# Moving small steps between engines around the recurrent stage and the attention of a two-layer hybrid trunk

## The reference, cut to what matters

```python
# mixer A: per query the 256 best admissible keys by an index score, then attention over these
score = where(admissible, sum_h w[q,h] * relu(q_idx . k_idx), -inf)
_, idx = lax.top_k(score, topk)        # of equal scores the earlier key wins
p = softmax(where(valid, q_lat . c_kv[idx], -inf))
o_lat = p @ c_kv[idx];  y_a = o_lat @ w_uv
# mixer B: gated delta rule over chunks of 64 rows
S = S * exp(g_last) + k^T (u - w S);   o = (q exp(g)) S + attn (u - w S)
y_b = rmsnorm(o) * silu(z)
# both
h = h + concatenate([y_a, y_b]) @ w_out
```

## Time and profile before

| what | value |
|---|---|
| median of three runs | 2384.43 us |
| the profiled execution's own time | 2382.29 us |
| its span in the trace | 2380.3 us |
| PE busy | 2322.6 us, 98% |
| DVE, ACT, POOL busy | 1654.0, 1022.7, 534.0 us |
| granted TensorE clock, mean | 0.993 of full |

### The profile page before, as it was taken

How to read it: one execution, slowest core, us unless ns; L and a number is a source line. 1 busy time by engine, 2 the same in 40 slices (tenths; PEclk the granted TensorE clock), 3 DMA queues, 4 the chain that set the end, 5 groups by cost and what they waited for, 6 DMA issues and landing times.

```text
span 2380.3 us, 33751 instructions
## 1 busy us (share of the span) xinstructions
PE 2322.6 (98%) x12906; PEld 1835.8 (77%) x12906; DVE 1654.0 (69%) x2671; ACT 1022.7 (43%) x1807; POOL 534.0 (22%) x504
## 2 busy tenths in 40 slices
PE   9999999988999999999999999989999999999998
PEld 6587778864577888888888867767878888888887
DVE  5388787788656977676755587546688777765557
ACT  5323325755633433333333454456343333333344
POOL 5026544311100234333330000000005333331000
PEclk9999999999999999999999999999999999999999
DMA  6121100010043355455596621101335455468663
GB/s 185 47 71 53 45 27 20 3 37 1 28 141 134 116 186 170 157 177 161 192 323 194 195 62 49 49 28 54 115 119 198 149 171 177 143 207 302 205 194 126
DMA packets 236271, 298.26 MB, mean 125 GB/s; under 512 B 13424, under 2 KB 175232, under 8 KB 227024
## 3 DMA queue, kind: packets, MB, share of 16 engines
q1 hardware_dynamic: 220848, 207.66, 28.3%
q0 software_dynamic: 15264, 88.45, 9.9%
HBM read 206.95 MB, written 88.60 MB: 124 GB/s over the span
## 4 chain that ended last, share of the span: by engine, by line
PE 89%; DVE 6%; ACT 3%; issue 2%; POOL 0%; DVEq 0%; ACTq 0%; POOLq 0%
PE ps L378 25%; PE ps L380 25%; PE ps L379 25%; PE ps L3208 1%; PE ps L3228 1%; PE ps L3196 1%; ACT d_p L1723 1%; PE ps L2539 1%; DVE met L2311 1%; PE ps L2010 1%; PE ps L2553 1%; PE ps L1964 1%; PE ps L2548 1%; PE ps L1537 1%; PE ps L2590 0%
## 5 line engine op out<-in xcount | busy, mean ns | idle before, releaser
L378 PE MATMUL ps<-uhi,whi 128*128 128x512 f32 x608 | 246.8, 406 | 7.6 <-DVE ulo L537 3.4
L378 PE MATMUL ps<-q_T,whi 128*128 128x512 f32 x640 | 249.2, 389 | 1.6 <-ACT upr L862 1.6
L380 PE MATMUL ps<-q_T,wlo 128*128 128x512 f32 x640 | 249.0, 389 | 0.0
L379 PE MATMUL ps<-q_T,whi 128*128 128x512 f32 x640 | 249.0, 389 | 0.0
L378 PE MATMUL ps<-q_B,whi 128*128 128x512 f32 x608 | 238.9, 393 | 2.4 <-DVE q_B L537 2.4
L378 PE MATMUL ps<-ahi,whi 128*128 128x512 f32 x616 | 240.4, 390 | 0.0
L380 PE MATMUL ps<-ahi,wlo 128*128 128x512 f32 x616 | 239.7, 389 | 0.0
L379 PE MATMUL ps<-alo,whi 128*128 128x512 f32 x616 | 239.7, 389 | 0.0
L380 PE MATMUL ps<-uhi,wlo 128*128 128x512 f32 x608 | 237.2, 390 | 0.0
L379 PE MATMUL ps<-ulo,whi 128*128 128x512 f32 x608 | 237.0, 390 | 0.0
L380 PE MATMUL ps<-q_B,wlo 128*128 128x512 f32 x608 | 236.6, 389 | 0.0
(11 more groups left out here) (479 smaller groups left out, 4988.0 us busy)
## 6 DMA issues: line engine op xcount, KB each, us to landing
wraw<-in_ffn_w_gate_dram SPq DMA_DIRECT2D x44, 512.0 KB, 5.2
wd<-in_ffn_w_down_dram POOLq DMA_DIRECT2D x22, 1024.0 KB, 7.3
w_sums<-wd POOLq DMA_DIRECT2D x22, 1024.0 KB, 4.9
wraw<-w_sums SPq DMA_DIRECT2D x40, 512.0 KB, 3.8
araw<-act_sums SPq DMA_DIRECT2D x40, 512.0 KB, 4.7
wraw<-in_ffn_w_down_dram SPq DMA_DIRECT2D x30, 512.0 KB, 5.9
araw<-acts SPq DMA_DIRECT2D x30, 512.0 KB, 6.4
wraw<-in_ab_w_in_dram SPq DMA_DIRECT2D x24, 512.0 KB, 3.8
```

The costliest lines, as they stand in the source:

```text
L378: nc.tensor.matmul(dst, wh, xh, start=start, stop=False, **kw)
L379: nc.tensor.matmul(dst, wh, xl, start=False, stop=False, **kw)
L380: return nc.tensor.matmul(dst, wl, xh, start=False, stop=stop, **kw)
```

## The change

Five things are done, all in layer 0.

1. Gate steps: in turn -1 three of PE's eight `z` steps move from before the middle of the turn to after level 3's first half, after `turn_a` and after level 4. In the last tile half the order over k is 2, 0, 1, 3 to 7, and `z_done` is released one step earlier.
2. Counts: two counts of turn -1 move from place 2 to place 3; one moves from turn 5 to turn 6; in turn 7 three, none, one, one, two become one, two, two, one, one, and place 1 comes after `add_state` instead of before.
3. Ties: step 1 of `select_mask` leaves VectorE. GpSimd does it (`ties(b)`), for block 2 ahead of its first `dg` and for the others ahead of the `dg` of 2, 4, 5, 8 and 9. The threshold's nine links are cut in three parts at pairs 0 and 1.
4. Moves: in the second group of 16 units ScalarE moves the odd groups of transposes too.
5. Splits: those of the first half of the output projection leave `out_act` and `out_dve` and go to the last two rounds of the attention, mixer B's pieces first and in a place of their own (`y_far`, 16 KB); PE takes k in the order 4 to 7, 0 to 3.

```diff
+        y_far = [at(f"y_far{n}", [P, 4, HALF], off * KB, F32R) for n, off in (("hi", 188), ("lo", 196))]
+        def y_order(layer, h):
+            return (4, 5, 6, 7, 0, 1, 2, 3) if (layer, h) == (0, 0) else range(KT)
+        def y_high(act, layer, y, i):
+            h, j = divmod(i, KT)
+            k = y_order(layer, h)[j]
+            act.activation(y_piece(layer, h, 0, k), y(k)[:, rows_of(h)], ACT.Copy).then_inc(S("y_high"), 1)
...
 def out_act
-            for name, value in waits:
-                act.wait_ge(*after(name, value))
-            for i in range(KT):
-                high(i)
+            if layer == 1:
+                for name, value in waits:
+                    act.wait_ge(*after(name, value))
+                for i in range(KT):
+                    y_high(act, layer, y, i)
             for i in range(2 * KT + 1):
                 if i < 2 * KT:
                     w_high(act, Tile(first[(kind, 0)] + i + 2))
+                if layer == 0 and i == 0:
+                    for name, value in waits:
+                        act.wait_ge(*after(name, value))
...
-        IN_PERIOD = {-2: (2, 0, 0, 0, 0, 4), -1: (2, 3, 2, 2, 0, 3), 0: (2, 2, 1, 1, 0, 0), 1: (2, 2, 1, 1, 0, 1),
-                     2: (2, 1, 1, 1, 0, 2), 3: (1, 1, 1, 1, 0, 3), 4: (1, 1, 0, 1, 0, 3), 5: (1, 1, 0, 1, 0, 4),
-                     6: (2, 2, 2, 2, 2, 3), 7: (3, 0, 1, 1, 2, 0)}
+        IN_PERIOD = {-2: (2, 0, 0, 0, 0, 4), -1: (2, 3, 0, 4, 0, 3), 0: (2, 2, 1, 1, 0, 0), 1: (2, 2, 1, 1, 0, 1),
+                     2: (2, 1, 1, 1, 0, 2), 3: (1, 1, 1, 1, 0, 3), 4: (1, 1, 0, 1, 0, 3), 5: (1, 1, 0, 1, 0, 3),
+                     6: (2, 3, 2, 2, 2, 3), 7: (1, 2, 2, 1, 1, 0)}
...
 def z_steps
-            for k in range(k0, k1):
+            for j in range(k0, k1):
+                k = (2, 0, 1, 3, 4, 5, 6, 7)[j] if q == 5 else j
...
-            elif (q, k1) == (5, 5):
+            elif (q, k1) == (5, 4):
                 last.then_inc(S("z_done"), 1)
...
 def gdn_dve
-                search(n, 1)
+                if n < NB - 1:
+                    search(n, 1)
...
+                if n == NB - 1:
+                    search(n, 1)
                 if O_:
                     invert(dve, n - 1)
...
 def att_act
+        ALL_BY_ACT = range(len(AU) // 4, len(AU) // 2)
...
                     att_move(act, 0, i - 2, copy)
+                    if i - 2 in ALL_BY_ACT:
+                        att_move(act, 1, i - 2, copy)
...
+                if i == len(AU):
+                    act.wait_ge(*after("at_masked", len(AU)))
+                    act.wait_ge(S("g_y"), NB)
+                    for j in range(3):
+                        y_high(act, 0, y_ab, j)
+                if i == len(AU) + 1:
+                    act.wait_ge(*after("at_y", AS // 2))
+                    for j in range(3, KT):
+                        y_high(act, 0, y_ab, j)
...
 def att_dve
+                if p == AP_:
+                    for j in range(3):
+                        y_low(dve, 0, y_ab, j)
+                if p == 1:
+                    select_threshold(dve, 1)
                 if p < AP_:
                     masked(2 * p + 1)
...
+                if p == AP_:
+                    dve.wait_ge(*after("at_pv", AS - 1))
+                    for j in range(3, KT):
+                        y_low(dve, 0, y_ab, j)
...
+        TIES_AFTER = {2: 3, 4: 4, 5: 5, 8: 6, 9: 7}
+
         def att_pool(pool):
+            def ties(b):
+                i, w = b - 2, WID[b]
+                if i:
+                    pool.wait_ge(S("fin_c"), 2 * i)
+                else:
+                    pool.wait_ge(S("thr_step"), 9)
+                pool.tensor_scalar(hT[:, 1, 0:w], scb(b), thr[:, i:i + 1].bitcast(F32), FAR, ALU.is_equal,
+                                   ALU.mult).then_inc(S("fin_a"), 1)
+
+            ties(2)
             for s in range(AS):
+                if s in TIES_AFTER:
+                    ties(TIES_AFTER[s])
```

More of the change, by code:

```diff
@@ L1841, in out_dve @@
         def out_dve(dve, kind, layer, y, norm, waits=()):
-            def low(i):
-                k, rows = i % KT, rows_of(i // KT)
-                dve.wait_ge(S("y_high"), 16 * layer + i + 1)
-                dve.tensor_tensor(y_op[i // KT][1][:, k, :], y(k)[:, rows], y_op[i // KT][0][:, k, :].bitcast(F32),
-                                  ALU.subtract).then_inc(S("y_ready"), 1)
-            for i in range(KT):
-                low(i)
+            if layer == 1:
+                for i in range(KT):
+                    y_low(dve, layer, y, i)
             for i in range(2 * KT):
@@ L2348, in select_keep, with select_threshold @@
             dve.tensor_tensor(mag[:, :], mag[:, :], thr[:, :], ALU.bitwise_or).then_inc(S("sel_kept"), 1)
-        def select_threshold(dve):
-            n_ = [0]
+        def select_threshold(dve, part):
+            n_ = [3 * part]
             def link(ins):
@@ L2701, in gdn_pe @@
                     turn_a(n + 2)
+                if n == -1:
+                    z(n, 1)
                 if S_:
@@ L3303, in mask_steps @@
             done = sum(each[:q - first_])
-            return [(2 * g + 2 + r // 6, r % 6) for r in range(done, done + each[q - first_])]
+            return [(2 * g + 2 + r // 6, r % 6) for r in range(done, done + each[q - first_]) if r % 6 != 1]
         def att_dve(dve):
@@ L3335, in att_dve @@
                     invert_sums(p // 2 - 1)
-                if 1 <= p <= AP_:
+                if 1 <= p <= AP_ and 2 * p - 2 not in ALL_BY_ACT:
                     att_move(dve, 1, 2 * p - 2, copy)
+                if p == AP_:
[3 more added lines that the diff above has]
+                    select_threshold(dve, 1)
                 if p < AP_:
                     masked(2 * p + 1)
-                if 1 <= p <= AP_:
+                if 1 <= p <= AP_ and 2 * p - 1 not in ALL_BY_ACT:
                     att_move(dve, 1, 2 * p - 1, copy)
```

62 lines of the change are left out of this document (33 added, 29 removed).

## The result

The changed kernel took 2367.9 us, median of four runs (2366.25 to 2372.35), against 2384.3 us for the kernel before beside it (2382.23 to 2384.69). The ratio is 0.9936, 95% interval 0.9919 to 0.9953: faster by 0.6%. Measured twice more beside other kernels it gave 2370.9 us (0.9947, 0.9931 to 0.9962) and 2368.9 us (0.9926, 0.9909 to 0.9944). The forecast was 2369.0, range 2361 to 2378. The profiled execution of the change took 2372.35 us.

What follows compares the result with a forecast made beforehand. PE was taken as the bound, busy 2322.6 of 2380.3 us. Terms 4.6 + 1.4 + 1.6 + 3.0 + 1.0 + 3.6 = 15.2 us off the 2384.4 median gave 2369.2 us, range 2361 to 2378.

Steps and rivals of the forecast that it cites:

- Part 1: Gate steps and counts of turn -1: 0.5 us of idleness and 4.1 us of slow clock gained, 4.6 us.
- The first rival: Turn -1: the clock falls all the same, because of 1.5 us waiting before `make_w`; 2373.3 us, chance 0.27.
- Part 2: Turn 7: with fewer counts ahead of `add_out`, PE's waits for the normed output and the state go, 1.4 us.
- Part 3: Six tie marks to GpSimd at 2.0 ns an element, covered by 5.3 us before the scan; no cost.
- The slower rival: A GpSimd mark outlasts its 5.3 us cover and its scan waits, each further us lost six times; chance 0.04.
- The rival of a held VectorE: GpSimd's marks, 8.4 us, hold VectorE up and take back the attention groups' gains and more; 2378 us, chance 0.05.
- Parts 3 and 4: Attention: tie marks to GpSimd and moves to ScalarE relieve VectorE, 5.6 us over the first, second and 576-to-612 stretches.
- Second group 3.0 of 3.8 us idle: Attention's second 16 units: VectorE falls to 21.9 us, ScalarE rises to 23.3, PE becomes the bound; 3.0 us gained.
- 576 to 612: 1.0: Attention from 576 to 612 us: two marks of 1.4 us leave VectorE, 1.0 us of PE's 1.74 idle gained.
- First group: 1.0 and the clock 0.6: Attention's first units: 1.0 of 5.25 us idle gained, and 0.6, half of what the 0.93 clock costs.
- The rival that ScalarE sets the pace: Attention's second group: ScalarE's moves delay its exponentials, the group gives 0, clock dips stay; 2376 us, chance 0.12.
- Part 5: Earlier output projection splits: PE's 2.41 us wait goes and 1.4 us of slow clock at its head; 3.6 us.

Runs made afterwards that it cites:

- the counts alone: Kernel before the change with only the two counts of turn -1 moved from place 2 to 3, gate steps left: 2381.7 us, ratio 0.9989.
- doubled marks: Changed kernel with each of GpSimd's six tie marks made twice, same result: 2377.0 us, ratio 0.9970.
- the marks alone: Changed kernel with the middle groups' moved copies back on VectorE, tie marks still on GpSimd: 2369.7 us, ratio 0.9932.
- the copies alone: Changed kernel with tie marks back on VectorE and the threshold in one piece, copies still on ScalarE: 2368.9 us, ratio 0.9933.

## Why the prediction was right, and where its steps were not

The total is right, and half of its terms. It is right in part by luck. The profiles of before and after differ by 9.7 us, not 15.2; and 2369.0 lies between the change's two groups of runs, where none of the sixteen fell. By the lowest runs, where the clock falls least, the parts give: gate steps and counts 1.4 (2376.89 to 2375.53), splits 3.7 (to 2373.15 alone), turn 7 2.1 (2368.35 to 2366.25), marks and copies 3.8 (2370.03 to 2366.25): 11.0 us of a difference of 10.6 between the lowest runs. These shares hold to 1 or 2 us, since the stretch in layer 1 is in them. By stages at clock 1.00 they are 1.5, 2.5, 2.2 and 3.0 us, 9.2 in all. The rest of the 12.8 to 16.4 us between the medians goes with the mean clock: most runs of before lie 4 to 8 us above its lowest, by its one profile in turn -1 and behind; over half of the change's lose 4 us, by its three profiles at the attention's start.

- **Part 1, 4.6 us: right**, 4.66. TensorE's busy time in turn -1 fell by 3.15 us (23.60 to 20.45) and its idleness by 1.5. The forecast had 4.1 and 0.5. The wait before `make_w` was taken too long, because the sum of TensorE's work beside the four counts has one gate step where two stand, and 2.6 us where the timeline has 4.2. The first rival, the clock falling all the same (0.27), holds for the counts alone; none of the eleven profiles with the gate steps moved shows it.
- **Part 2, 1.4 us: right at its place**, 1.5 in the two waits named. The count moved from turn 5 to 6, costed at nothing, gave another 0.7; the last 0.8 of the stage's 2.95 is the tail of turn -1's slow stretch, outside the window that the forecast read.
- **Part 3, the marks: almost hidden, but by a wrong price and a wrong cover.** Taken 2.0 ns an element; measured 3.3 and 0.3 us each. The rate lies within the bounds of 582 ns a mark and 4.1 ns an element. The cover of 5.3 us, read at one block, was the wrong measure: the `need` step, which VectorE makes ahead of the scan, waits for the mark, and the margins are 1.0 to 3.7 us in one profile; in the other two the 640-wide mark is late by 0.28 us, which the prediction had named as a sign of being wrong. The slower rival's price of a late mark (one for one) was too low: doubled marks cost 9.0 us in two groups where VectorE waited 5.3. The rival of a held VectorE is refuted: with the longer marks on GpSimd its masked scores keep their mean, 883 ns against 882 with the marks on VectorE. The Trainium skill (SBUF — State Buffer, "Who interferes with whom") agrees: a VectorE operation with at most one input in SBUF, outside the two-port modes, doesn't contend with GpSimd. The Trainium skill's other rule, that one-input elementwise work runs at about line rate on GpSimd (GPSIMD Engine Reference, "Engine selection"), put a mark at an estimated 0.4 to 1 us; the trace has 1.6 to 3.7.
- **Parts 3 and 4, 5.6 us: the step that failed.** At clock 1.00 they give 3.0. "Second group 3.0 of 3.8 us idle": it became 1.8 us shorter (26.88 to 25.08), though VectorE's busy time near it came out close to the forecast, 22.3 us of 29 (21.9), and ScalarE's at 22.1 (23.3). Neither engine is full, and TensorE still waits there for the maxima three times, 1.7 us in all: a mean load below TensorE's doesn't end waits that come from the order inside a pair. "576 to 612: 1.0": 0.9 (37.12 to 36.24). "First group: 1.0 and the clock 0.6": 0.3 at clock 1.00, and for the clock the sign was wrong. The prediction let the clock only improve; it fell to 0.57 there, and cost the profiled run more than both parts had won. The wait for `nmx`, forecast at some 3 us, is 3.4 only beside 20 us of slow clock; at clock 1.00 it is 7.6 us with the marks alone and 6.8 with the copies alone.
- **The rival that ScalarE sets the pace** (0.12) is refuted for the second group: none of TensorE's waits from 543 to 572 us is for ScalarE. It was half right elsewhere: at the attention's start ScalarE is late.
- **Part 5, 3.6 us: right**, 2.48 and 1.59, VectorE's margin 0.16 us where 0.1 was read, the fourth weight tile no limit. That the 1.4 us of clock belong to the splits is not shown: one kernel without them has clock 1.00 there.

The three errors had different signs: turn 7's stage gave 1.5 us more, the attention 2.6 to 7 less, and between the medians the clock gave more than the two profiles show.

## What to carry to other kernels

Read the clock as a resource with more than one outcome: list the runs by mean granted clock before trusting a median or a single profile, and hold a stage against a variant that ran it at the same clock. Filling TensorE's waits with its own work (gate matmuls here, with two counts moved) gave the steadiest gain; a balance of busy shares promises more than it gives, since waits inside a pair stay. Where work goes to a slower engine, find the first instruction that waits for it, read the margin at every block and in more than one profile, then double the work once to see what lateness costs. A window of fixed times drifts off its stage when an earlier one gets shorter; measure from the same point to the same point.

## What was not expected of the hardware

- A GpSimd compare-and-multiply over 128 partitions, fp32 in SBUF with a per-partition scalar, took 3.3 ns an element and 0.3 us (1585 ns for 384, 3704 for 1024), four to five times VectorE's 414 to 748 ns.
- TensorE's clock doesn't do the same each time at one place. Behind 521 us it was down for 17 to 20 us in the three profiled runs of the change. Other kernels that run the same groups with the same waits up to there, to 0.01 us, had it down for 3 us or not at all. With a wait of 0.4 or 0.5 us instead of 1.3 one kernel fell for 3 us and one for 20. What decides stays open.
- While the clock was down, TensorE's waits shrank (7.0 to 7.3 us of idleness in the attention against 10.6 to 12.2 in kernels at 1.00): a slower TensorE gives the others time, so a fall costs less than its matmuls' lengthening. An estimate from the change's third profile: 131.0 us busy against 124.3 at 1.00 with the marks alone, 6.7 us more, for 4.6 in the first group's length.
